# Moving instructions on VectorE, ScalarE, TensorE and GpSimd in a two-block transformer kernel, and one weight sum from DMA to VectorE

## What is computed

```
hn = rmsnorm(h, g)
gu = hn @ w_gate_up                     # 1024 x 5632
act = silu(gu[..., :D_FF]) * gu[..., D_FF:]
h = h + act @ w_down                    # 2816 x 1024 (block two: 0.5 * rmsnorm of it)
```

## Time and profile before

| | us |
|---|---|
| median of 3 runs | 1270.5 |
| the profiled execution, its own time | 1271.37 |
| its span | 1269.6 |
| TensorE busy | 1253.5 (99%) |
| VectorE busy | 1042.7 (82%) |
| ScalarE busy | 804.0 (63%) |
| GpSimd busy | 192.4 (15%) |

### The profile page before, as it was taken

The page is one execution under the profiler, slowest core; times in us unless marked ns, Lnnn a source line. Parts: engine busy times, 40 slices in busy tenths (PEclk is TensorE's granted clock), DMA queues, the critical chain, the costliest instruction groups (busy, mean ns, idle before and its releaser), DMA issues.

```text
span 1269.6 us, 15538 instructions
## 1 busy us (share of the span) xinstructions
PE 1253.5 (99%) x5897; PEld 1028.9 (81%) x5897; DVE 1042.7 (82%) x1035; ACT 804.0 (63%) x986; POOL 192.4 (15%) x224
## 2 busy tenths in 40 slices
PE   9999999999999999999999999999999999999998
PEld 7888878888888878788778888788888877788886
DVE  6766689999799996767899997999977568999984
ACT  6674576665576664645766664766656466766662
POOL 6142130110001100102201101111001003301100
PEclk9999999999999999999999999999999999999999
DMA  9537498997649955568979978389745535999931
GB/s 333 174 100 231 133 313 254 268 270 248 201 151 255 269 168 180 188 226 215 320 249 245 271 251 255 116 237 274 219 166 173 184 125 168 315 286 262 266 135 44
DMA packets 143002, 277.32 MB, mean 218 GB/s; under 512 B 8992, under 2 KB 39896, under 8 KB 142928
## 3 DMA queue, kind: packets, MB, share of 16 engines
q1 hardware_dynamic: 120192, 229.67, 51.6%
q0 software_dynamic: 22288, 45.54, 19.7%
q10 hardware_dynamic: 448, 1.12, 0.2%
HBM read 275.24 MB, written 1.05 MB: 218 GB/s over the span
## 4 chain that ended last, share of the span: by engine, by line
PE 77%; DVE 12%; issue 4%; ACT 3%; DMA 3%; POOL 0%; DVEq 0%; SPq 0%; ACTq 0%
PE B L2102 14%; PE B L2104 14%; PE B L2103 14%; DVE w_lo L1359 7%; PE B L2558 6%; PE B L2560 6%; PE B L2559 6%; PE T L2102 3%; PE T L2104 3%; PE T L2103 3%; DMA VD<-in_ffn_w_gu 2%; DVE VD L1378 1%; DMA Z<-in_ffn_w_gu 1%; ACT w_hi L1082 1%; ACT w_hi L768 1%
## 5 line engine op out<-in xcount | busy, mean ns | idle before, releaser
L1359 DVE TENSOR_TENSOR w_lo<-w_raw,w_hi 128x2048 fp32r<-128x2048 f32 x129 | 296.5, 2299 | 87.5 <-ACT w_hi L768 87.2
L768 ACT ACTIVATE w_hi<-w_raw 128x2048 fp32r<-128x2048 f32 x129 | 247.1, 1918 | 102.7 <-PE B L2560 60.3
L2102 PE MATMUL B<-w_hi,xt_lo 128*128 128x512 f32 x652 | 260.5, 400 | 5.1 <-DVE w_lo L1359 2.1
L2104 PE MATMUL B<-w_hi,xt_hi 128*128 128x512 f32 x652 | 254.7, 391 | 0.0
L2103 PE MATMUL B<-w_lo,xt_hi 128*128 128x512 f32 x652 | 254.0, 390 | 0.0
L2558 PE MATMUL B<-w_hi,act_lo 128*128 128x512 f32 x440 | 172.5, 392 | 0.8 <-DVE w_lo L1359 0.4
L2560 PE MATMUL B<-w_hi,act_hi 128*128 128x512 f32 x440 | 171.4, 390 | 0.0
L2559 PE MATMUL B<-w_lo,act_hi 128*128 128x512 f32 x440 | 171.3, 389 | 0.0
L2102 PEld LDWEIGHTS B<-w_hi,xt_lo 128*128 128x128 f32 x652 | 122.4, 188 | 36.1 <-issue 6.2
L2104 PEld LDWEIGHTS B<-w_hi,xt_hi 128*128 128x128 f32 x652 | 122.4, 188 | 26.4
L2103 PEld LDWEIGHTS B<-w_lo,xt_hi 128*128 128x128 f32 x652 | 122.6, 188 | 23.3
(11 more groups left out here) (330 smaller groups left out, 2110.0 us busy)
## 6 DMA issues: line engine op xcount, KB each, us to landing
w_raw<-in_ffn_w_down SPq DMA_DIRECT2D x88, 512.0 KB, 5.8
Z<-in_ffn_w_gu SPq DMA_DIRECT2D x64, 512.0 KB, 8.1
w_raw<-in_ffn_w_gu SPq DMA_DIRECT2D x48, 512.0 KB, 5.2
nat<-in_ffn_w_gu SPq DMA_DIRECT2D x32, 512.0 KB, 7.8
QT<-in_ffn_w_gu SPq DMA_DIRECT2D x32, 512.0 KB, 7.0
Z<-in_ffn_w_gu POOLq DMA_DIRECT2D x32, 512.0 KB, 8.8
w_raw<-in_conv_w_in SPq DMA_DIRECT2D x24, 512.0 KB, 4.7
w_raw<-in_w_down SPq DMA_DIRECT2D x22, 512.0 KB, 6.6
```

What stands on the lines that cost most here:

```text
L768: act.activation(whi[home(u)][:, :], raw[slot][:, :], ACT.Copy).then_inc(w_hi, 1)
L1359: dve.tensor_tensor(wlo[home(u)][:, :], src, whi[home(u)][:, :].bitcast(F32), ALU.subtract).then_inc(w_lo, 1)
L2102: pe.matmul(bank[:, :], lo[:, k, x], whi[s][:, c], start=first, stop=False, skip_group_check=more)
L2104: return pe.matmul(bank[:, :], hi[:, k, x], whi[s][:, c], start=False, stop=last, skip_group_check=more)
```

## The change

The fourth sum T4 is made by VectorE in all four pairs, and stands behind the low part of Da (in pair 0 behind that of P7). Around it several calls change places: result C12, the low part of Db and T1; `act_out(1)` and T1; the start of a network on VectorE and ScalarE; a low part of the convolution; `o_norm(1)` and `heads_lo(0)`; a cumulated sum's low part and a weight's; the rounds that turn `h` for the shared key and value product; and the order of some down and output products on TensorE. GpSimd issues 20 DMAs fewer, two of 512 KB in each of ten pairs. No instruction of TensorE is added or removed.

```diff
-SUMS = ((1, "T1"), (1, "T2"), (2, "T1"), (2, "T2"), (3, "T1"), (3, "T2"), (3, "T4"))
-ADDED_T4 = (1, 2)
+SUMS = tuple((_p, _t) for _p in range(1, SQUARES) for _t in ("T1", "T2", "T4"))
+ADDED_T4 = ()
@@ ScalarE, start of a network
                 block("P1", 0)
+                act.wait_ge(rstd, 2 * ST[stat] + 2)
+                gate_of(0, u0 + OP["N0b", 0], PAIR[0] if f else F0)
                 act.wait_ge(sx_ok, f + 1)
                 act.wait_ge(w_used, u0 + OP["N0b", 0] + 1)
                 act.activation(yhi[:, :, :], xsum, ACT.Copy).then_inc(sx_hi, 1)
-                act.wait_ge(rstd, 2 * ST[stat] + 2)
-                gate_of(0, u0 + OP["N0b", 0], PAIR[0] if f else F0)
@@ VectorE, the forgetting term
-            split_at(7)
             dve.wait_ge(c_hi, 1)
             low = slice(64, CK)
             dve.tensor_tensor(cT[low, :], B[3][low, 0:S], cT[low, :].bitcast(F32), ALU.subtract).then_inc(c_out, 1)
+            split_at(7)
@@ VectorE, a network
-                if f == 0:
-                    total = x_total(reader)
-                else:
+                if f:
...
+                weights("N1b")
+                if f == 0:
+                    total = x_total(reader)
                 x_sums(total)
-                weights("N1b")
-                block("P1", 0)
                 dve.wait_ge(rstd, 2 * ST[stat] + 2)
                 act_of(0, PAIR[0] if f else F0)
+                block("P1", 0)
...
                 block("P3", 0)
+                block("P7", 0)
                 weight_sum("T4", f, 0)
-                block("P7", 0)
                 weights("D0")
                 block("P4", 0)
                 result("C22", 0)
                 weights("D1")
                 result("C12", 0)
+                act_out(1)
                 weight_sum("T1", f, 1)
-                act_out(1)
                 result("C11", 0)
                 for p in range(1, SQUARES):
...
                     block("P6", p)
-                    if p not in ADDED_T4:
-                        weight_sum("T4", f, p)
                     block("P3", p)
                     block("P7", p)
                     act_out(2 * p)
                     weights("Da", p - 1)
+                    if p not in ADDED_T4:
+                        weight_sum("T4", f, p)
                     act_out(2 * p + 1)
...
                     result("C12", p)
+                    weights("Db", p - 1)
                     if p + 1 < SQUARES:
                         weight_sum("T1", f, p + 1)
-                    weights("Db", p - 1)
                     result("C11", p)
...
                 if kv:
                     kv_round_lo(1)
+                if kv:
+                    kv_round_lo(2)
                 split_at(u0 + FFN_UNITS)
                 if kv:
-                    kv_round_lo(2)
                     kv_round_lo(3)
@@ VectorE, the convolution and the differential attention
-            conv_taps(2)
             conv_lo(0)
             conv_lo(1)
+            conv_taps(2)
...
             o_sum(1)
+            o_norm(1)
             heads_lo(0)
-            o_norm(1)
@@ TensorE, end of a network
-                down("Db", SQUARES - 1, (lambda: kv_round(2)) if kv else (lambda: None))
+                d, u = down_ready("Db", SQUARES - 1)
+                down_part(d, u, 0, 0)
+                down_part(d, u, 0, 1)
+                if kv:
+                    kv_round(2)
+                down_part(d, u, 1, 0)
                 if kv:
                     kv_round(3)
-                d, u = down_ready("DN2", 0)
-                down_part(d, u, 0, 0).then_inc(tok0_done, 1)
-                down_part(d, u, 0, 1).then_inc(tok0_done, 1)
+                d1, u1 = down_ready("DN2", 0)
+                down_part(d1, u1, 0, 0).then_inc(tok0_done, 1)
+                down_part(d1, u1, 0, 1).then_inc(tok0_done, 1)
+                down_part(d, u, 1, 1).then_inc(w_used, 1)
@@ TensorE, the output product of the attention
+            out_heads(0, 4, 1)
             heads_pair(3)
-            for k in (4, 5):
-                out_heads(0, k, 1)
+            out_heads(0, 5, 1)
+            out_heads(1, 4, 1)
             pe.wait_ge(ao_lo, 4)
```

More of the change, by code:

```diff
@@ L2634, in ffn @@
                     kv_round(1)
-                down("Db", SQUARES - 1, (lambda: kv_round(2)) if kv else (lambda: None))
+                d, u = down_ready("Db", SQUARES - 1)
[4 more added lines that the diff above has]
+                down_part(d, u, 1, 0)
                 if kv:
                     kv_round(3)
-                d, u = down_ready("DN2", 0)
-                down_part(d, u, 0, 0).then_inc(tok0_done, 1)
-                down_part(d, u, 0, 1).then_inc(tok0_done, 1)
+                d1, u1 = down_ready("DN2", 0)
+                down_part(d1, u1, 0, 0).then_inc(tok0_done, 1)
+                down_part(d1, u1, 0, 1).then_inc(tok0_done, 1)
+                down_part(d, u, 1, 1).then_inc(w_used, 1)
+                d, u = d1, u1
                 down_part(d, u, 1, 0).then_inc(tok1_half, 1)
@@ L2868, in _ @@
                 out_heads(1, k, 0)
+            out_heads(0, 4, 1)
             heads_pair(3)
-            for k in (4, 5):
-                out_heads(0, k, 1)
[L2872 to L2878, removed]
+            out_heads(0, 5, 1)
+            out_heads(1, 4, 1)
+            pe.wait_ge(ao_lo, 4)
+            for half in range(2):
+                for k in (6, 7):
+                    out_heads(half, k, 0)
+            for k in (6, 7):
+                out_heads(0, k, 1)
+            for k in (5, 6, 7):
                 out_heads(1, k, 1)
```

## The result

After the change the kernel takes 1293.3 us (median of 5 runs, 1292.6 to 1294.0), before it 1270.9 (5 runs): ratio 1.0174, 95% interval 1.016 to 1.0188. The forecast was 1291.8. The profiled execution took 1293.28 us, its span is 1291.5, which is 21.9 more than before.

A forecast was written before the change was run, and what follows sets the result against it. TensorE, busy 99% of the span, was taken as the bound, so only its waits count. Bodies +22.0, T3 +1.5, other places and starts -2.25 make +21.3 on 1271.4: 1292.7, median 1291.8 us; own range 1286 to 1297, 8-in-10 range 1279 to 1300.

The forecast's parts named there:

- The body: P5 of pair 0 to N2a in each network: +5.0 us, 3.4 and 3.6 in networks 1 and 2; sum +22.0.
- VectorE's first forced wait: Da's low part must follow Da's high part, 6.34 us from P6's start, with VectorE's queue closed behind it.
- the 1.60 a cycle: P6 to next P6 in pairs 1 to 3: 32.42 us against 30.82, two cycles a network, 3.2 us.
- totals don't bind: Against the rival that only VectorE's totals count, a pair costing 0.18: about 1271.5 us, no change, chance 0.06.
- Pair 0 and pair 0 to 1: T4 behind P7's low part: D0 0.8 us late; act_out(1) ahead of T1: 1.15 us more, per network.
- T3: T3's DMAs issued later, behind the moved T1: 0.3 us a network, +1.5; rival of late T3, 1300 us, chance 0.12.
- The places outside: Network starts and other moved calls outside the bodies: -2.25 us together, between -5 and +1.
- N1b's waits: Network starts, N1b's low part ahead of `x_sums`: -0.3 us each in networks 2, 3, 4; +0.5 in network 0.
- The turned `h`: Shared key and value product: fourth round of transposes earlier, but TensorE held by the second-last round's low part; +0.6 us.
- the ends of networks 1 and 2: First token's sums 6 matmuls earlier on TensorE, so the transposes behind do not wait: -0.6 us in all.
- What would show it: Signs: pairs of 32.3 to 32.6 us, idle VectorE before P7's and Da's low parts, TensorE's waits some 35 us.

The follow-up runs named there:

- t1_behind_db: Kernel before with one move: Db's low part ahead of T1 on VectorE in pairs 1 to 3, T4 of pairs 1 and 2 still by DMA; 1287.3 us.
- p6_t1_behind_db: Kernel before with T4 by VectorE in all pairs, behind P6's low part in pairs 1 to 3, and Db's low part ahead of T1; 1292.6 us.
- t4_behind_p6: Kernel before with T4 by VectorE in all four pairs, in pairs 1 to 3 right behind P6's low part; 1272.4 us, ratio 1.0009.
- p6_pair0: As t4_behind_p6, plus T4 of pair 0 behind P7's low part and act_out(1) ahead of T1; 1283.0 us.
- pair0_only: Kernel before with only T4 of pair 0 behind P7's low part and act_out(1) ahead of T1; T4 of pairs 1 and 2 by DMA; 1288.2 us.
- t4_before_da: Changed kernel with T4 of pairs 1 to 3 between P7's low part and act_out, ahead of the wait for Da's high part; 1297.2 us.
- t4_alone: Kernel before with only T4 made by VectorE in all four pairs, in pairs 1 to 3 behind Da's low part; 1285.5 us.
- outside_only: Kernel before with all of the change except T4, the pairs and pair 0; 1270.6 us, ratio 0.9992.
- after_t4_dma: Changed kernel with T4 of pairs 1 and 2 made by two adding DMAs again, all moved calls staying moved; 1293.5 us.

## Why the prediction was right

**The body, +5.0 a network: the size is right, 4.96 on average of networks 0, 3, 4, 3.36 and 3.54 in networks 1 and 2 (forecast 3.4 and 3.6).** Sum 21.8 for 22.0. A pair took 32.37 to 32.43 for 32.42; VectorE's busy time was 30.85 for 31.00. All of this was worked out from VectorE's first forced wait.

**Its cause: half right.** The text gave the 1.60 a cycle to the added sum behind Da, and said of the other move that "T1 and Db, and what stands between, only change places; the sum of the queue is the same". The sum is the same, and the move still costs as much as the added sum: t1_behind_db +15.7 us in the bodies, p6_t1_behind_db +21.0 over t4_behind_p6. T4's place alone makes the pair 32.5 us long, T1's move alone 32.2 and more, and both together, in the changed kernel, 32.4. They are two cycles side by side, of 32.4 and 32.1 us, over much the same instructions of VectorE. That the number came out right is luck in this: the cycle that was seen is the longer one, by 0.24 (the rows of 883.99 and 881.83 above), and nothing in the prediction had compared the two. Had only T1 moved, the same reasoning would have said no change and missed by 16 us. In the trace of before, T1 filled the wait for Db's high part, so that VectorE shows no idle time there. T1 on VectorE, Db's high part on ScalarE and Db's low part on VectorE, network 3, pair 2, before:

```profile
899.31 2.28 DVE L1378 TENSOR_TENSOR KT<-Z 128x2048 f32<-128x2048 f32 x1
```

```profile
899.32 1.92 ACT L768 ACTIVATE w_hi<-w_raw 128x2048 fp32r<-128x2048 f32 x1 [3.37 <-PE B L2560]
```

```profile
901.50 2.28 DVE L1359 TENSOR_TENSOR w_lo<-w_raw,w_hi 128x2048 fp32r<-128x2048 f32 x1
```

T1 and Db's high part run side by side, and Db's low part starts 0.26 behind the end of the latter (901.24).

**That totals don't bind: right.** 2.20 us more a pair cost 0.1, 5.4 or 12.9 us in the bodies by place alone (behind P6, P3, Da). From each of the three some 3 us are already taken off, the waits for T4's DMAs that go in networks 1 and 2; in a network without such waits the cost is 0.64, 1.64 or 3.2 us. Behind P6, VectorE was made 2% busier (20.1 of 1042.7 us) at the same time of the kernel within 0.2%. The prediction's rows showed 0.74 of VectorE's 2.02 us of free time, ahead of Da's low part; the rest stood ahead of P3's and P7's.

**Pair 0 and pair 0 to 1: right.** D0 is 0.7 late (0.8 forecast, drawn wait 1.06 for "about 1.1"), the first Da 2.0 in all (0.8 and 1.15 forecast); alone, in p6_pair0, 2.2 in all. It depends on T4 in pair 1: with the DMAs (pair0_only) the same moves cost 3.0 to 4.2 a network.

**T3, +1.5 forecast, nothing found.** T1 for pair 2 of network 3 ended at 888.48 and P7's high part began at 899.42, 10.94 later (10.9 worked out), with no wait for a DMA. The median landing was 8.2 us, 8.8 before, at a DMA share of 0.77 in the pair for 0.96. In pairs 1 to 3 of all networks the second DMA landed 8.7 to 10.7 us behind T1's end: the 12.0 us from which it would cost were not reached, but it is not far. In t4_before_da one landed too late, by 0.28. The rule of the Trainium skill, "DMA: Bandwidth & Descriptors", section "Anatomy of one DMA", gave the right term, nothing, with a duration that the row again shows to be far off: its 3.2 us against 8.2.

**The places outside, -2.25 forecast, +0.1 found in the trace.** This +0.1 is the difference of two single traces, and the stretch ahead of network 0's body alone differs by 0.45 us between kernels in which it is the same (193.70 in t1_behind_db, 194.15 in t4_alone). The runs of outside_only give -1.0 (-2.2 to +0.1). N1b's waits went in networks 2 to 4. From N1a to P5 of pair 0, networks 2 and 3 are 0.6 and 0.5 shorter, where 0.3 each was forecast. In network 4, -0.3 was forecast and +0.9 came: N1b's high part stands behind four squares of the norm on ScalarE (the row of 1115.95), VectorE now waits 1.43 for it ahead of `x_sums`, and P2 waits 1.25 for the gated product. Before, `x_sums` ran under this wait, as T1 did under Db's. The prediction had seen this for network 0 alone (+0.5 forecast, +0.6 found). The turned `h` cost 0.5 (0.67 before, 1.18 after), and the ends of networks 1 and 2 gained 0.2 each of the 0.3 forecast. The errors here and at T3 have opposite signs: together -0.75 was forecast and +0.1 found. That they leave only this much is luck too.

**What would show it.** Pairs, D0, P5 and P6, no wait of ScalarE for a DMA at P4, and waits of 33.5 us for "some 35" were found. Idle time ahead of P7's low part was not; all of it stood at Da's. One reading of the earlier trace rows was wrong without changing the sum: the low parts of weights are 4.6 of the 9.8 us of waits listed before, the largest share but not most. For the Trainium skill's advice in "Perfetto Trace Analysis", section "Optimizing Scalar/DVE Operations", to move work off a saturated VectorE: after_t4_dma does that and stays at 1293.5, and t4_behind_p6 does the opposite to the kernel before and stays at its time. VectorE was not saturated here.

## What to carry to other kernels

Before moving an instruction on an engine that serves a busier one, list each place where its queue must wait for something that the busier engine releases, also the places where it shows no idle time, and ask what work stands between this wait and the next. Each gives a cycle of its own, and work that moves from ahead of such a wait to behind it costs its whole time less the spare (for T4 here 2.20 less 0.70, and 0.10 behind TensorE's wait), though the engine's total stays the same. If the first move makes a cycle long, others of the same length hide beneath it; undo the moves one by one from the kernel before, not from the kernel after.

## What the runs showed that had not been expected

T4's two adding DMAs were worth less than thought: with P6's low part just in time for TensorE they release P4's high part 12.2 and 12.3 us behind P6's start (after_t4_dma, pair0_only), which lets VectorE idle for 2.0 to 2.1 us. VectorE's sum has no such dependence: in t4_behind_p6 the five bodies agree within 0.03 us (118.41 to 118.44), with the DMAs they spread from 117.8 to 119.4.
